# Expert up-projections as 512-wide products, with the row tiles dealt over TensorE's four column groups

## The reference

```python
def expert_block(args):
    xblk, e = args
    return (jax.nn.silu(xblk @ w1[e]) * (xblk @ w3[e])) @ w2[e]
...
lg = (xf @ wg + bg).astype(f32)                  # 4 groups
_, grp = lax.top_k(lg, 1)
...
top_p, top_i = lax.top_k(jax.nn.softmax(le_g, axis=-1), TOP_K_IN_GROUP)   # 2 of 8 experts
...
y = grouped_experts(xf, eid.reshape(-1), gate.reshape(-1), w1, w3, w2)
...
return x + g2 * hier_moe(h2, ...)
```

## Time and profile before

| | |
|---|---|
| Median of the runs | 1685.8 us |
| Span of the profiled execution | 1681.7 us (first to last instruction; mean granted clock 0.910) |
| What lies around it, by the median | 4.1 us |
| PE busy | 1338.6 us (80%), 12765 products and as many weight loads |
| DVE, ACT, POOL busy | 549.5, 129.5, 27.3 us |
| DMA | 613.31 MB, mean 365 GB/s |
| Experts' weights, first issue to last landing | 681.6 to 1667.6 us |
| Expert loop on PE | from 752.2 us on |

### The profile page before, as it was taken

The page is one execution under the profiler, slowest core; times in us unless marked ns, Lnnn a source line. Parts: engine busy times, 40 slices in busy tenths (PEclk is TensorE's granted clock), DMA queues, the critical chain, the costliest instruction groups (busy, mean ns, idle before and its releaser), DMA issues.

```text
span 1681.7 us, 28215 instructions
## 1 busy us (share of the span) xinstructions
PE 1338.6 (80%) x12765; PEld 836.4 (50%) x12765; DVE 549.5 (33%) x901; ACT 129.5 (8%) x283; POOL 27.3 (2%) x30
## 2 busy tenths in 40 slices
PE   5999999999999999997676676566576567566757
PEld 4665447754457854584443435335245244343434
DVE  4552563863555543432221121120121121122203
ACT  2001000111000100130000000000000000000000
POOL 0000000000000000010000000000000000000000
PEclk9999999999999999999987788788788788788778
DMA  9997885766658666959999999999999999999995
GB/s 397 428 427 288 329 339 237 266 263 268 267 200 337 263 263 250 374 234 413 425 426 427 425 428 425 426 426 426 425 428 426 426 426 427 426 426 426 426 428 222
DMA packets 44622, 613.31 MB, mean 365 GB/s; under 512 B 4896, under 2 KB 5168, under 8 KB 6736
## 3 DMA queue, kind: packets, MB, share of 16 engines
q1 hardware_dynamic: 42848, 604.00, 86.7%
q0 software_dynamic: 1072, 6.44, 0.9%
q10 hardware_dynamic: 576, 0.88, 0.1%
HBM read 609.21 MB, written 2.10 MB: 364 GB/s over the span
## 4 chain that ended last, share of the span: by engine, by line
DMA 47%; PE 46%; issue 3%; DVE 3%; SPq 0%; POOL 0%; ACT 0%; DVEq 0%
DMA Zpad<-in_exp_w 22%; DMA ring<-in_exp_w 17%; PE W L624 16%; PE W L616 7%; DMA ring<-in_stream 6%; PE M L1015 5%; PE W L930 5%; DMA tail<-in_exp_w 3%; PE A L1031 2%; PE W L906 2%; PE W L987 2%; PE M L600 1%; DVE tail L1323 1%; PE W L590 1%; PE W L974 1%
## 5 line engine op out<-in xcount | busy, mean ns | idle before, releaser
L624 PE MATMUL W<-ring,buf_h 128*128 128x512 f32 x704 | 306.2, 593 | 0.5 <-DMA ring<-in_stream 0.5
L1323 DVE SCALAR_TENSOR_TENSOR tail<-ring,small,tail 128x512 f32<-128x512 f32 x300 | 225.6, 752 | 10.5
L1015 PE MATMUL M<-ring,g1b 128*32 128x128 f32 x4096 | 149.5, 309 | 78.6 <-DMA ring<-in_exp_w 75.4
L624 PEld LDWEIGHTS W<-ring,buf_h 128*128 128x128 f32 x704 | 132.2, 190 | 160.5 <-issue 160.2
L1015 PEld LDWEIGHTS M<-ring,g1b 128*32 128x32 f32 x4096 | 130.4, 125 | 94.8 <-DMA ring<-in_exp_w 87.0
L1793 DVE SCALAR_TENSOR_TENSOR tail<-tail,M 128x128 f32<-128x128 f32 x32 | 9.2, 288 | 420.0 <-ACT tail L1233 420.0
L1256 DVE TENSOR_TENSOR consts<-A,tail 32x512 f32<-32x512 f32 x128 | 87.9, 686 | 178.8 <-PE A L1031 175.7
L1015 PE MATMUL M<-Zpad,g1b 128*32 128x128 f32 x2048 | 80.8, 324 | 55.8 <-issue 55.8
L616 PE MATMUL W<-buf_h,ring 128*128 128x256 f32 x512 | 112.0, 379 | 0.3 <-DMA ring<-in_stream 0.3
L1031 PE MATMUL A<-Zpad,tail 128*32 128x512 f32 x512 | 76.8, 728 | 41.5 <-DMA Zpad<-in_exp_w 37.7
L1015 PEld LDWEIGHTS M<-Zpad,g1b 128*32 128x32 f32 x2048 | 69.3, 132 | 71.6 <-issue 68.0
(11 more groups left out here) (293 smaller groups left out, 939.4 us busy)
## 6 DMA issues: line engine op xcount, KB each, us to landing
ring<-in_stream SPq DMA_DIRECT2D x88, 2048.0 KB, 10.2
ring<-in_exp_w SPq DMA_DIRECT2D x88, 2048.0 KB, 38.6
Zpad<-in_exp_w SPq DMA_DIRECT2D x64, 2048.0 KB, 33.5
PPY<-in_exp_w SPq DMA_DIRECT2D x24, 2048.0 KB, 32.3
tail<-in_exp_w SPq DMA_DIRECT2D x16, 2048.0 KB, 46.2
Zpad<-in_early SPq DMA_DIRECT2D x8, 1536.0 KB, 10.6
buf_x<-in_x SPq DMA_DIRECT2D x2, 1024.0 KB, 7.0
buf_h<-in_x POOLq DMA_DIRECT2D x1, 2048.0 KB, 13.5
```

The lines of the kernel that those rows point to most:

```text
L624: ins = pe.matmul(dst[:, tt * 512:tt * 512 + 512], hT[:, kk, tt * P:tt * P + P], w[:, 512 * k:512 * k + 512], start=(kk == 0), stop=(kk == ...
L1015: ins = pe.matmul(M[32 * c:32 * c + 32, 512 * w13:512 * w13 + 128], XT[:, kk, 32 * q:32 * q + 32], w[:, 512 * k + 128 * c:512 * k + 128 * ...
L1323: ins = dve.scalar_tensor_tensor(acc, w, cs[:, kk:kk + 1], acc, ALU.mult, ALU.add)
```

## The change

The row tiles are dealt over the four column groups. Row tile `kk` goes to the group `j = kk % 4` with all 512 hidden columns as one moving operand; a row tile is one product and not four. Each group of 32 partitions then holds, for all 512 hidden columns, a sum over four of the sixteen row tiles only. ACT copies these partial sums (128 x 512) to SBUF, in `part`; PE multiplies each 128 columns of `part`, as the stationary operand, by `sel`, a 0/1 matrix of 128 x 32 with a one where the partition modulo 32 is the column. This adds the four groups and turns the result in one: hidden columns on partitions, tokens along the row, the layout that the down-projection wants. It is done for `w1` behind the third half (`h1T`) and for `w3` behind the fourth (`h3T`). Tanh and the products of DVE then work on the turned values, and DVE writes `hTs` itself, so that the transpose and the copy to `hTs` are gone. `sel`, which served another step with 20 columns, has 32 now. The turned gate matrix moves to PSUM columns of its own, and the wait for `gt_ready` stands ahead of the first sum of `q` = 1.

```diff
-for _n, _w in (('ident', P), ('tri', P), ('ones', P), ('sel', NX), ('selr', 64), ('iota', 32),
+for _n, _w in (('ident', P), ('tri', P), ('ones', P), ('sel', 32), ('selr', 64), ('iota', 32),
...
-        hh, ee, aa = (tmp[:, 768 + 128 * i:896 + 128 * i] for i in range(3))
+        part = tmp[:, 768:1280]
+        ee, aa = tmp[:, 1536:1664], tmp[:, 1664:1792]
+        h1T, h3T, turned_G = M[:, 1024:1152], M[:, 0:P], M[:, 1280:1536]
...
+            def sum_and_turn(dst):
+
+                for c in range(4):
+                    ins = pe.matmul(dst[:, 32 * c:32 * c + 32], part[:, P * c:P * c + P], const('sel'),
+                                    start=True, stop=True)
+                return ins
...
                                 for k in range(8):
                                     kk = 8 * hf + k
-                                    for c in range(4):
-                                        ins = pe.matmul(M[32 * c:32 * c + 32, 512 * w13:512 * w13 + 128],
-                                                        XT[:, kk, 32 * q:32 * q + 32],
-                                                        w[:, 512 * k + 128 * c:512 * k + 128 * c + 128],
-                                                        start=(kk == 0), stop=(kk == KT - 1))
+                                    j = k % 4
+                                    ins = pe.matmul(M[32 * j:32 * j + 32, 512 * w13:512 * w13 + 512],
+                                                    XT[:, kk, 32 * q:32 * q + 32], w[:, 512 * k:512 * k + 512],
+                                                    start=(kk < 4), stop=(kk >= KT - 4))
                                 ins.then_inc(half_used, 1)
-                        pe.wait_ge(sem["hh_ready"], 4 * it + q + 1)
-                        if q == 1:
-                            pe.wait_ge(sem["gt_ready"], it + 2)
-                        pe.transpose(M[:, 1024:1152], hh, ident).then_inc(sem["hh_turned"], 1)
+                                if (w13, hf) == (1, 0):
+                                    if q == 1:
+                                        pe.wait_ge(sem["gt_ready"], it + 2)
+                                    pe.wait_ge(sem["part_copied"], 8 * it + (2 * q + 1))
+                                    sum_and_turn(h1T).then_inc(sem["h_turned"], 1)
+                        pe.wait_ge(sem["part_copied"], 8 * it + (2 * q + 2))
+                        sum_and_turn(h3T).then_inc(sem["h_turned"], 1)
                         pe.wait_ge(sem["hT_ready"], 4 * it + q + 1)
...
+                        act.wait_ge(half_used, PER_GROUP * it + (PE_BASE + 6 * q + 2))
+                        act.activation(part, M[:, 0:512], ACT.Copy).then_inc(sem["part_copied"], 1)
+                        act.wait_ge(sem["h_turned"], 8 * it + (2 * q + 1))
+                        act.activation(ee, h1T, ACT.Tanh, scale=0.5).then_inc(sem["e_ready"], 1)
                         act.wait_ge(half_used, PER_GROUP * it + (PE_BASE + 6 * q + 4))
-                        act.activation(ee, M[:, 0:128], ACT.Tanh, scale=0.5).then_inc(sem["e_ready"], 1)
-                        act.wait_ge(sem["hh_turned"], 4 * it + q + 1)
-                        act.activation(hTs, M[:, 1024:1152], ACT.Copy).then_inc(sem["hT_ready"], 1)
+                        act.activation(part, M[:, 512:1024], ACT.Copy).then_inc(sem["part_copied"], 1)
...
-                        dve.scalar_tensor_tensor(aa, ee, 1.0, M[:, 0:128], ALU.add, ALU.mult).then_inc(
+                        dve.scalar_tensor_tensor(aa, ee, 1.0, h1T, ALU.add, ALU.mult).then_inc(
                             sem["dve_loop_step"], 1)
                         dve.wait_ge(sem["dve_loop_step"], loop_step_no())
-                        dve.scalar_tensor_tensor(hh, M[:, 512:640], 0.5, aa, ALU.mult, ALU.mult).then_inc(
-                            sem["hh_ready"], 1)
+                        dve.wait_ge(sem["h_turned"], 8 * it + (2 * q + 2))
+                        dve.scalar_tensor_tensor(hTs, h3T, 0.5, aa, ALU.mult, ALU.mult).then_inc(
+                            sem["hT_ready"], 1)
```

More of the change, by code:

```diff
@@ L193 @@
     "r_pv_done", "m_cols_read", "m_args_ready", "x1_ready", "router_done", "wr_ready", "hid_parts", "hid_summed", "g2_summed", "g2_ready", "wout_part", "part_ready", "first_ready", "counted", "y_ready", "y_turned", "yT_ready", "mask_ready",
-    "places_done", "g_ready", "y_added", "gathered", "g_turned", "xt_act", "xt_dve", "gt_ready", "round_shifted", "hh_ready",
-    "hh_turned", "hT_ready", "y_copied", "scattered", "x_loaded0", "x_loaded1", "late_loaded", "c_tanh", "x_squared", "gains_ready",
+    "places_done", "g_ready", "y_added", "gathered", "g_turned", "xt_act", "xt_dve", "gt_ready", "round_shifted", "part_copied",
+    "h_turned", "hT_ready", "y_copied", "scattered", "x_loaded0", "x_loaded1", "late_loaded", "c_tanh", "x_squared", "gains_ready",
     "gate_tanh_m", "gate_tanh_r", "n_gate_tanh", "f_abs", "f_exp", "f_one", "f_ln", "gelu_arg", "gelu_tanh",
@@ L214, in constants @@
     put('selr', p[:, None] % 64 == np.arange(64)[None, :])
-    put('sel', p[:, None] % 32 == np.arange(NX)[None, :])
+    put('sel', p[:, None] % 32 == np.arange(32)[None, :])
     put('iota', np.tile(np.arange(1, 33), (P, 1)))
@@ L1037, in _ @@
                             scatter(it)
-                            pe.wait_ge(sem["hT_ready"], 4 * it + 1)
                             for tt in range(TT):
-                                ins = pe.transpose(M[:, 1024 + tt * P:1024 + tt * P + P],
+                                ins = pe.transpose(turned_G[:, tt * P:tt * P + P],
                                                    tmp[:, 256 + 128 * tt:384 + 128 * tt], ident)
@@ L1231, in _ @@
                     for q in range(4):
+                        act.wait_ge(half_used, PER_GROUP * it + (PE_BASE + 6 * q + 2))
+                        act.activation(part, M[:, 0:512], ACT.Copy).then_inc(sem["part_copied"], 1)
+                        act.wait_ge(sem["h_turned"], 8 * it + (2 * q + 1))
+                        act.activation(ee, h1T, ACT.Tanh, scale=0.5).then_inc(sem["e_ready"], 1)
                         act.wait_ge(half_used, PER_GROUP * it + (PE_BASE + 6 * q + 4))
-                        act.activation(ee, M[:, 0:128], ACT.Tanh, scale=0.5).then_inc(sem["e_ready"], 1)
-                        act.wait_ge(sem["hh_turned"], 4 * it + q + 1)
-                        act.activation(hTs, M[:, 1024:1152], ACT.Copy).then_inc(sem["hT_ready"], 1)
+                        act.activation(part, M[:, 512:1024], ACT.Copy).then_inc(sem["part_copied"], 1)
                         if q == 0:
                             act.wait_ge(sem["g_turned"], it + 1)
-                            act.activation(GT, M[:, 1024:1280], ACT.Copy).then_inc(sem["gt_ready"], 1)
+                            act.activation(GT, turned_G, ACT.Copy).then_inc(sem["gt_ready"], 1)
                         if q == 3:
```

## The result

The changed kernel takes 1670.88 us (median of 4 runs, 1668.65 to 1673.08), the kernel before 1685.35 us beside it; the ratio is 0.991, with a 95% interval of 0.9898 to 0.9922. In a second series on one chip it was 1667.98 us against 1684.98 us, ratio 0.9896 (0.9881 to 0.9912). Of the rivals, "the loop's code stays resident" had named 1671 us.

A forecast was written before the change was run, and what follows sets the result against it. Weight transfers were taken as the bound, ending with eight DMA engines made late by code fetches. Fewer packets -7.4, loop start +0.8, end 0 gave -6.6 us: 1679.2 us, own range 1676 to 1684, with other cases 1673.5 to 1686.0.

The forecast's parts named there:

- the loop's code stays resident: Rival: PE's buffer holds the shorter loop body, up to 84 fewer packets, 1671 us; chance 0.08.
- the transfer is the bound: Expert loop: weight transfers decide, DMA share 1.01; PE has some 86 us of slack in two iterations.
- width by itself gives nothing: Up-projections: 64 products 512 wide take 7.3 us an expert against 7.4 us now, no change.
- the sixteen engines end apart because of the code's packets: End of kernel: eight DMA engines lag by 17.5 us, put down to 94 instruction fetches at 1.49 us each.
- The records of an iteration: Loop on PE: 530 products an iteration, with the loads 1060 records in place of 2476.
- The last expert's chain: End: copy, sums and down-projections finish by 1667.0 us, still ahead of the last transfer; cost nothing.
- the lower bound: Late engines at the end: at 1.12 us a packet they finish 5.6 us sooner, not 7.4.
- the count of packets left: Loop's instruction queue: 7 packets an iteration in place of 12, 40 fewer in all, worth 7.4 us.
- The start of the loop: Second transfer gap, 790 us: two experts' extra work +2.7 us, less a 1.91 us stall gone, +0.8 us.
- The bound of 3.7: Start of the loop: +3.7 us if the stall stays and one of the sums runs at half clock.
- I had bounded it at 1.5: End: up to +1.5 us if the clock is low in the last down-projection, 1.92 becoming up to 3.4 us.
- The base: Whole kernel: the execution's median lies 4.1 us over the profiled span, left as it is: 1675.1 becomes 1679.2 us.

The follow-up runs named there:

- five kernels: The kernel before, and the changed kernel with up-projection products cut to 128 columns, 256, or mixes of 128 with 512 or 256: 1681.73 to 1689.47 us.
- the second profile: Profile of the changed kernel run once more, unaltered: span 1664.6 us; that series measured 1667.98 us, ratio 0.9896 to the kernel before.

## Why the prediction was wrong

**What held.** That the transfer is the bound and PE's time is worth nothing: PE became busier by 14 us in two iterations and the kernel faster. That width by itself gives nothing: 0.114 us a record at the full clock, as estimated, and the kernels with narrower products lie with their packets, not with their width. That the sixteen engines end apart because of the code's packets: where the packets go the lag goes, and in the others it grows with their number, at 1.49 us for each on one of eight: five kernels, the one before among them, give 1.45 to 1.53. The records of an iteration, 1060, to the record. The last expert's chain: hidden. A packet's own time was worked out as 1.12 us from a share that is rounded to 0.7%; the 94 packets in the trace take 1.06 us each in the mean. It bore on the lower bound alone.

**The step that failed** is the count of packets left: "as packets are whole I take 7 in an iteration, 5 fewer, 40 in all". Of 94 packets 89 went, not 40. 89 x 1.49 / 8 = 16.6 us; by the second profile, where the start is like that of before, the last product begins 17.1 us sooner (1650.52 against 1667.63) and the span is 17.1 us shorter. The path from the packets to the time was right, and so was the price of one; their number was not, since the prediction put a loop that is fetched anew where there is one that stays. The working treated the fetches as proportional to the code with a constant for the jump, which holds above the limit: 9 packets in an iteration with 1572 records, 12 with 2476. Below it the number is zero. The limit lies between 1444 and 1572 records (the waits and register instructions among them, some forty in an iteration of these kernels' programs, are not in the count), and the changed loop is well under it. Where the limit comes from, and whether it is PE's buffer that keeps the code, no run shows.

I had this as a rival, at 1671 us and a chance of 0.08. What I held against it was a poor argument: that PE's 12 packets exceed the body's 10.1 shows that a loop that is too long fetches past its end, and says nothing of a loop that fits. The argument for it, that the loops of DVE and ScalarE run without any packet (two iterations of the changed kernel without one now show it), was the one to follow; and the Trainium skill's 2048 instructions for PE's buffer ("Runtime: NRT & Kernel Launch", Instruction fetch mechanics) had pointed there. The runs agree with it in that there is a limit far above two blocks of 256, but not in the figure: 1572 records, with the forty others, are fetched anew each time. The sentence of the same page in the Trainium skill, that crossing a block is mostly hidden, is contradicted for a kernel bound by its transfers: 70 packets go with a lag of 13.1 us.

**The start of the loop** was put at +0.8, bounded by 3.7. Measured from first to second issue: 3.1 us more in one execution and 1.2 us less in the other. At one clock it is 2.6 us for the sums less 1.9 for the stall, +0.7, so the term was right; what moved the two executions is the clock, in three groups of the one and in none of the other, and in one group of the kernel before. The bound of 3.7 took the half clock in a sum and the stall kept; the clock fell in down-projections and in the scatter instead, and the stall is gone. At the end of the span the clock cost 2.7 us once and nothing the other time; I had bounded it at 1.5 for the down-projection alone and left out the products behind it.

**The base.** I carried 4.1 us from the profiled span to the median. The runs of the changed kernel have 1.8 us around the span (1673.08 against 1671.3), so the profiled execution of before was simply among its fastest; this moves nothing in a difference, but made the profile's own difference (10.4 us) smaller than that of the medians (14.5 us).

## What to carry to other kernels

In a loop that is bound by its transfers, look at the instruction queue in the DMA answer before anything else: if it has packets in every iteration, the loop's code is being fetched over and over, on the engines that bring the data. Bring the body under the size at which the packets stop (here 1444 records of products and loads on PE run without them, 1572 do not); wider products, fewer records for the same columns, are one way. And look at whether the DMA engines end together: a stretch at share 0.50 before the end says that half of them are late, and packets of code that come with it are the first thing to suspect. The gain comes in one step when the loop gets short enough; here it was not in proportion to the code saved.

## What the runs showed of the hardware

- A packet of 16 KB of code costs the queue of weights about 1.5 us on its engine (1.45 to 1.53 over five kernels), more than its own 1.06 us. That the packets run on the eight late engines is inferred from the share of 0.50 and its going with the packets; no row shows the engine of a packet.
- The jump from 6 to 70 packets lies between 1444 and 1572 records in a loop on PE; above it an iteration costs 9, 10, 11, 12 and 13 packets for 1572, 1828, 2084, 2476 and 2596 records (the totals over the 8 iterations, rounded up; the last is 12.6). With the packets come PE's waits on issue: 28, of 69.7 us in all, from 800 to 1645 us in the kernel before, and none in the changed one.
- The granted clock fell to its lower level (1.2 GHz) in part of single groups of products at the start of the loop in one execution (5.34 us for 32 records of 512 columns) and stayed at 2.4 GHz in another of the same kernel (3.64 us), both behind PE's idle time of 0.56 to 2.38 us, the same in both. Single times of one kernel are 4 us apart; the clock at the start of the loop and at its end is a part of that (4.3 and 2.7 us between these two executions).
